# Two swiglu layers: four plain column pairs, then pairs of gate and up columns by seven half-size products

## The reference

```
h = rmsnorm(x, g_pre_ffn)                       # over the 1024 channels
g, u = split(h @ w_gu)                          # w_gu: 1024 x (2816 + 2816)
x = x + 0.5 * rmsnorm((silu(g) * u) @ w_down, g_post_ffn)   # w_down: 2816 x 1024
```

## Time and profile before

| what | value |
|---|---|
| median of three runs | 2426.96 us (2425.76 to 2429.64) |
| profiled execution, its own time | 2429.99 us |
| its span, first to last instruction | 2428.2 us |
| TensorE busy | 2366.4 us, 97% |
| VectorE busy | 1330.4 us, 55% |
| ScalarE busy | 1064.6 us, 44% |
| GpSimd busy | 233.4 us, 10% |
| DMA, mean over the span | 95 GB/s |

### The profile page before, as it was taken

One profiled execution on the slowest core, in us unless ns is written; L12 is line 12 of the kernel. 1 busy time (PEld: TensorE's weight loads), 2 busy tenths in 40 slices (PEclk: granted clock), 3 DMA queues, 4 the chain that ended last, 5 costly groups with the idle time before them and its releaser, 6 DMA issues.

```text
span 2428.2 us, 30842 instructions
## 1 busy us (share of the span) xinstructions
PE 2366.4 (97%) x12214; PEld 1941.6 (80%) x12214; DVE 1330.4 (55%) x2135; ACT 1064.6 (44%) x1759; POOL 233.4 (10%) x189
## 2 busy tenths in 40 slices
PE   8999999999999999999999999999999899999998
PEld 7888888777777788888887667989987677888987
DVE  5533436788654345432435866735645776753643
ACT  4323224455432334322323556614634785742642
POOL 0100100322102010100100300001001100000100
PEclk9999999999999999999999999999999999999999
DMA  4323223211122132323222214536532012744641
GB/s 145 100 87 109 95 87 100 85 53 53 61 70 72 55 117 70 104 86 114 88 86 88 86 44 130 148 104 160 136 96 74 29 47 72 172 115 125 150 122 64
DMA packets 72864, 230.68 MB, mean 95 GB/s; under 512 B 8080, under 2 KB 16528, under 8 KB 72464
## 3 DMA queue, kind: packets, MB, share of 16 engines
q1 hardware_dynamic: 66672, 206.68, 26.2%
q0 software_dynamic: 6048, 22.02, 5.5%
HBM read 226.57 MB, written 2.10 MB: 94 GB/s over the span
## 4 chain that ended last, share of the span: by engine, by line
PE 84%; DVE 6%; ACT 5%; issue 3%; DMA 2%; POOL 0%; POOLq 0%; SPq 0%; DVEq 0%; ACTq 0%
PE bank L2145 21%; PE bank L2149 21%; PE bank L2147 21%; PE bank L2163 3%; PE bank L2167 3%; PE bank L2165 2%; DMA wraw<-in_stream 2%; PE bank L2328 2%; ACT whi L2449 2%; DVE wlo L2791 1%; PE bank L2290 1%; PE bank L2335 1%; PE bank L2236 1%; PE bank L2232 1%; PE bank L2234 1%
## 5 line engine op out<-in xcount | busy, mean ns | idle before, releaser
L2791 DVE TENSOR_TENSOR wlo<-wraw,whi 128x1024 fp32r<-128x1024 f32 (+3 forms) x462 | 518.2, 1126 | 530.9 <-ACT whi L2449 529.6
L2449 ACT ACTIVATE whi<-wraw 128x1024 fp32r<-128x1024 f32 (+3 forms) x462 | 434.9, 948 | 472.6 <-PE bank L2149 374.6
L2145 PE MATMUL bank<-hhi,whi 128*128 128x512 f32 x1288 | 515.2, 400 | 6.6 <-ACT whi L2449 4.6
L2149 PE MATMUL bank<-hhi,wlo 128*128 128x512 f32 x1288 | 504.2, 391 | 1.6 <-DVE wlo L2791 1.5
L2147 PE MATMUL bank<-hlo,whi 128*128 128x512 f32 x1288 | 503.6, 391 | 0.4 <-DVE hlo L2839 0.4
L2145 PEld LDWEIGHTS bank<-hhi,whi 128*128 128x128 f32 x1288 | 242.4, 188 | 61.2 <-issue 6.4
L2149 PEld LDWEIGHTS bank<-hhi,wlo 128*128 128x128 f32 x1288 | 242.1, 188 | 55.7 <-DVE wlo L2791 4.0
L2147 PEld LDWEIGHTS bank<-hlo,whi 128*128 128x128 f32 x1288 | 242.6, 188 | 49.6 <-DVE hlo L2839 2.5
L2145 PE MATMUL bank<-mhi,whi 128*128 128x512 f32 x448 | 177.2, 396 | 0.0
L2147 PE MATMUL bank<-mlo,whi 128*128 128x512 f32 x448 | 177.0, 395 | 0.2 <-DVE mlo L3145 0.2
L2149 PE MATMUL bank<-mhi,wlo 128*128 128x512 f32 x448 | 177.0, 395 | 0.0
(11 more groups left out here) (459 smaller groups left out, 4221.1 us busy)
## 6 DMA issues: line engine op xcount, KB each, us to landing
wraw<-in_stream SPq DMA_DIRECT2D x335, 512.0 KB, 3.5
wraw<-in_stream POOLq DMA_DIRECT2D x34, 512.0 KB, 6.0
wraw<-in_stream SPq DMA_DIRECT2D x32, 192.0 KB, 2.4
wraw<-in_stream SPq DMA_DIRECT2D x22, 256.0 KB, 2.6
rot_tables<-in_stream SPq DMA_DIRECT2D x8, 512.0 KB, 5.6
rot_tables<-in_stream POOLq DMA_DIRECT2D x8, 512.0 KB, 5.5
wraw<-in_stream SPq DMA_DIRECT2D x26, 128.0 KB, 2.0
wraw<-in_stream SPq DMA_DIRECT2D x8, 320.0 KB, 3.0
```

Of the source, the lines that this page charges most:

```text
L2145: pe.matmul(out, sh, xh, start=first, stop=False)
L2149: p = pe.matmul(out, sl, xh, start=False, stop=end and last)
L2449: act.activation(whi[j][:, 0:L], src[:, 0:L], F.Copy).then_inc(*hi.up(c))
L2791: dve.tensor_tensor(wlo[j][:, 0:L], src[:, 0:L], whi[j][:, 0:L].bitcast(f32), SUB).then_inc(*lo.up(c))
```

## The change

- **Swiglu columns.** Features 0, 1, 2 and 11 stay plain (eight columns, all at the start of the layer). The other eighteen go two at a time through seven products each: `GATED`, four blocks in the first half (starting at features 3, 5, 7, 9), five in the second (12, 14, 16, 18, 20). The four columns of a block are the gate and the up columns of two features.
- `token_sums` and the product loop (`by_seven`) are taken out of `mlp` so that both layers use them; the order of mlp's own steps stays. In `ffn`, pieces 0 to 3 of the token sums stand between the gates of features 0, 1, 2 and 11.
- **The finish of a block** is new: per block two more multiplications by `rb` on VectorE, three multiplications on GpSimd (two of them by `rb`), two silus and two high copies on ScalarE.
- **Down columns** are begun as in mlp: the first two are interleaved with the last two products.
- **The rotary steps** move to the second half's down columns, two before each of the columns 0 to 4. Their position load on SyncE now waits for the last q7's split and for the two buffers they use. `rot_tables` serves as a third weight buffer in both swiglu layers.
- **SBUF**: 96 bytes of padding (`to_128_bytes`), and `qk`, `dl`, `xch` allocated ahead of the odd-sized tensors; each tensor named above then starts at a multiple of 128 bytes.
- **The start**: the first weights are SyncE's first load, the columns' table and x's first tile are loaded from ScalarE's queue, the identity comes last; TensorE runs 20 matmuls of 128x128 on `ones` first.

```diff
+PLAIN, GATED = (0, 1, 2, 11), ((3, 5, 7, 9), (12, 14, 16, 18, 20))
...
+    def ffn(s, tag, gu, down_of):
+        lows[s], least = [], len(plan) + 2
+        for f in PLAIN:
+            col(tag + "g", gu + "g", f)
+            col(tag + "u", gu + "u", f)
...
+            seven(tag + "s", s, GATED[half], lambda f: quadrants([gu + "g"] * 2 + [gu + "u"] * 2, (f, f + 1) * 2), down,
+                  least)
...
+                g0, u0, g1, u1 = side_by_side(("h", s), *[(tag + c, n, 0) for n in range(2) for c in "gu"], fresh=s > 0)
+                g2 = run(feat([(tag + "g", 2, 0)], ("h", s)))
                 R.step()
+                token_sums(s, 0, guard)
                 gate(s, 0, g0, u0, afree)
                 gate(s, 1, g1, u1, afree)
+                u2 = run(feat([(tag + "u", 2, 0)], ("h", s)))
+                token_sums(s, 1, guard)
+                gate(s, 2, g2, u2, afree)
+                token_sums(s, 2, guard)
+                g3 = run(feat([(tag + "g", 11, 0)], ("h", s)))
+                token_sums(s, 3, guard)
+                state["held"] = True
+                u3 = run(feat([(tag + "u", 11, 0)], ("h", s)))
+                put("token_last", s, u3.end)
+                gate(s, 11, g3, u3, (("p_lo", ("last token", s)),))
...
+            elif name == "q3":
+                low()
+                u = silu_of[f, "up"]
+                put("glu_gate", key, "c12", q.i)
+                put("glu_second", key, q.i, u.i)
...
+                if half and n < 5:
+                    next(extra, None)
+                    next(extra, None)
...
+        sb("to_128_bytes", [128, 24])
...
                 if k == "init":
-                    sp.dma_start(cols[:, 0:ncols], t["cols"]).then_inc(ld["cols"], 16)
+                    fetch(raws[0])
+                    sp.dma_start(xa[:, 1, :], t["x"][:, 1, :]).then_inc(ldx[1], 16)
+                    fetch(raws[1])
...
-                    w.wait_ge(ld["ident"], 16)
                     w.wait_ge(*ones_set[0])
-                    pe.matmul(banks[0][0:1, 0:1], ident[:, 0:1], ones[:, 0:1], start=True, stop=True)
+                    for _ in range(20):
+                        pe.matmul(banks[0][:, 0:128], ones[:, :], ones[:, :], start=True, stop=True)
...
+                    act.dma_start(cols[:, 0:ncols], t["cols"]).then_inc(ld["cols"], 16)
+                    act.dma_start(xa[:, 0, :], t["x"][:, 0, :]).then_inc(ldx[0], 16)
```

More of the change, by code:

```diff
@@ L567, in gate, with token_sums @@
         q.free = (("v_lo", (s, f)),)
[L569 to L572 removed]
+    first, both = FT.slots
+    def token_sums(s, k, guard):
+        qs = [T.take(), T.take()]
+        for q, j in zip(qs, (k, k + 4)):
+            put("plain", s, j, q.i, (*q.was, *x_at[j]))
+        put("token_sums", s, k, qs[0].i, qs[1].i, (*first.free, *both.free), guard)
+        for q in qs:
+            q.free = (("combined", ("token", s, k, 4)),)
+        put("token_parts", s, k, guard)
+        first.free = both.free = (("p_hi", ("token", s, k)), ("p_lo", ("token", s, k)))
@@ L592, in ffn, with tile @@
+            def tile(n):
+                return feat([(tag + f"d{half}", n, k0) for k0 in (0, 8)], ("v", s, half))
+            begun = [tile(0), tile(1)]
+            h_end = multiplied(GATED[half], begun, iter(()))
+            while wait_lo:
+                low()
             if half:
@@ L1256, in multiplied @@
-        def multiplied(fs, tiles, afree):
-            def nothing():
-                pass
-            later = nothing
-            for f, name in products(fs):
-                if name == "down":
-                    next(tiles[0])
-                    next(tiles[0])
-                    later()
-                    later = nothing
-                    continue
-                at_once, then = product(f, name, (*afree, *open_sums["h", s].tok) if f == 12 else afree)
-                later()
-                if (f, name) == (4, "p5"):
-                    put("token_last", s, ("used", CH[(f"m{l}u", 3, 0)]))
-                at_once()
-                state["held"] = False
-                later = then
-                if f > 4:
-                    next(owed, int)()
-            next(tiles[1])
-            next(tiles[1])
-            later()
-            return ("used", CH[(f"m{l}s", fs[-1], "q3")])
+            if part == "c21":
+                q = T.take()
+                put("corner", key, part, b.i, q.i, (done, *q.was), free)
+                b.free = (("relu_sq", (key, part, "relu")),)
+            else:
+                put("corner", key, part, None, q.i, (), free)
```

318 lines of the change are left out of this document (210 added, 108 removed).

## The result

| | median us | ratio to before | 95% interval |
|---|---|---|---|
| before, same comparison | 2426.36 (2423.76 to 2432.35) | | |
| changed | 2451.48 (2449.62 to 2456.38) | 1.0103 | 1.0093 to 1.0113 |

The changed kernel is slower by 25 us; 2419 with a range of 2388 to 2438 was predicted.

The account below looks back on a forecast made before the run. The prediction took TensorE, busy for 97% of the span, as the bound: number of matmuls times the distance of their starts. Its terms summed to -8.4 us, from the median 2426.96 to 2419 us, range 2388 to 2438.

Parts of the forecast that it names:

- products: Swiglu columns: eight plain columns and nine blocks of seven products replace 44 plain columns; -31.8 us for two layers.
- placement: About 3000 matmuls of 512 tokens read data now aligned to 128 bytes and start closer together; -19 us.
- sums of tokens: Matmuls of 256 tokens on `thi` in the blocks may go from 0.1179 to 0.1200 us apart; +2.4 us.
- start: Kernel start: earlier first weights load and matmuls on `ones` bring the full rate forward; -3 us.
- join: Where swiglu's plain columns meet products, p5 and p6 wait behind token pieces and gates; +36 us.
- inside halves: TensorE's waits inside the blocks of the four swiglu halves; +4 us, bounds 0 and 10.
- ends of halves: At each half's end the last corner passes up to 0.9 us late, four times; +3 us.
- the rival with a chance of 0.08: The larger distance between matmul starts belongs to the place in SBUF, not the 32 bytes; 2436 us, chance 0.08.
- The rival on adding transfers: Adding transfers come late in the five-block halves, 3 us per half more; 2431 us, chance 0.07.
- The first rival: The swiglu join costs what mlp's does, +8 in place of +36; 2391 us, chance 0.20.
- VectorE as the bound: Rival: VectorE becomes the bound in the swiglu blocks, at 21.5 us per block; 2446 us, chance 0.10.

Follow-up runs that it names:

- pad_only: Kernel before with only the change's SBUF part: 96 bytes of padding and qk, dl, xch allocated earlier; 2423.4 us, ratio 0.9986.
- start_only: Kernel before with only the change's start: new load order and 20 matmuls on ones first; 2424.9 us, ratio 0.9992.
- data_low: Kernel before with the two halves of SBUF exchanged, stage tensors low and still 32 bytes past a multiple of 128; 2427.7 us, ratio 1.0006.
- holds_before_splits: Changed kernel with the weight splits of q7 and the next q1 put behind the holds of p5 and p6 in swiglu blocks; 2445.8 us, ratio 1.0086.
- pad_224: Kernel before with pad_only's layout but 224 bytes of padding in place of 96; 2409.2 us, ratio 0.9923.
- all_160: Kernel before as weights_160, with data also moved by 32 bytes, all but v_end; 2414.7 us, a single execution.
- weights_160: Kernel before with 224 bytes of padding, weights' buffers behind hhi and hlo and moved by 32 bytes; 2448.2 us, ratio 1.0090.

## Why the prediction was wrong

Its terms against what the traces and runs gave:

| term | predicted | measured | from |
|---|---|---|---|
| products | -31.8 | -31.8 | 0.1188 apart, a block 20.0 |
| placement | -19 | -3.5 | pad_only |
| sums of tokens | +2.4 | +1.9 | 0.1187, 2304 matmuls |
| start | -3 | -1.8 | start_only |
| join | +36 | +34.9 | 17.4 and 17.5 per layer |
| inside halves | +4 | +18.1 | 8.7 and 9.4 per layer |
| ends of halves | +3 | +3.4 | four columns, 0.85 late each |
| sum | -8.4 | +21.2 | 19.6 between the profiles |

The last three are read from the profile of the changed kernel, as the time between starts of matmuls beyond 0.1187 us on sums of tokens, 0.1199 on `hhi` and 0.2267 or 0.2327 for 512 tokens. The 1.6 us between the two sums are less than the scatter of single executions.

**The step that failed first** is placement: "All the tensors listed as 32 bytes past show the second distance", and from it "-19". The contrast was exact and the property named was one of several that went with it. The listed tensors differ from hhi by 32 bytes, by place, and by their remainder against the weights' buffers, and only the last one counts in these runs. The bound named for this term, "0, if the distance comes from the place", was nearly met (-3.5), but not because the place counts, and the rival with a chance of 0.08 gave 2436. That this lies nearer to the measured 2451 than the forecast does is luck: the rival's mechanism, the place, is refuted by data_low, and the number leaves out the waits below. Place and 32 bytes were taken as the only two alternatives. With 224 bytes the term would have been right in size: -18.

**The second** is "For four halves +4 us", the waits inside the halves, sized by the two waits that mlp had the earlier trace rows; they cost 18.1. A swiglu block asks more of the order than an mlp block: a product by rb, a silu and a product on GpSimd between two corner steps, with the same four temporaries. I costed these steps as VectorE's load (15.3 of 20.0 us, measured 14.0) and not as a chain through ScalarE's queue, where the split that waits for the row sum stands ahead of two holds. The rival on adding transfers, at 3 us per five-block half, named a link of this chain; the whole chain costs 9 per layer, and how much of it the transfer causes is open. What holds_before_splits shows is the order: 5.7 of the 18.1 us go when the splits of q7 and q1 stand behind the holds.

**The join was right** in mechanism, and in its sum partly by luck. rb's end to p5's whi: 25.2 predicted, 24.2 measured; to p6's whi 36.9 and 35.4; to p6's end 40.8 and 41.6. Inside the sum two shares were off and cancelled: TensorE waits 10.8 us in the second layer and not 16.7, and matmuls in windows with a granted clock of 0.52 and 0.64 cost 6.7 (17.5 less the waits) and not 1.3. The first rival (a join as short as mlp's) did not occur. The start lost part of its gain to its own second load, x's first tile, which reached ScalarE 1.0 us later than before.

**VectorE as the bound** did not come: 14.0 us of 20.2. Beside GpSimd a split takes 2.48 us (1065.35 in the second layer) in place of 1.22. That is 1.26 us more, beside a GpSimd instruction of 1.60 that had 1.38 still to run; the split at 1061.61, beside one that had 0.39 still to run, took 1.48. By what means the one delays the other is not shown.

All in all the products save 32 us and the join, the blocks and the ends of halves give 56 back. Of the 33 us between 2419 and 2451 the placement is 15.5 and the waits inside the halves 14.1. Some 5 us are the difference between the profiles' 19.6 and the medians' 25, which lies in the scatter of single executions.

## What to carry to other kernels

A contrast between groups of tensors is a hint of many properties at once. List them all (address by 32, 128, 256 and 512 bytes, place against the other operand, order, producer) before pricing one, and give the term a low chance when no run separates them. A faster form with more feeding steps is worth its saving only where the feeders' queues have slack in the right order: price each wait of an engine that works through one list in order as a chain, from the step that waits to everything queued behind it, and count the buffers, because with none to spare a step can be neither earlier nor later. Count the slow clock on the matmuls that follow long waits: here, after waits of 5.3 and 2.75 us, it was 6.7 of the join's 17.5 us in the second layer.

## What the runs showed of the hardware

- Matmuls of 512 columns in reduced fp32: in the runs where weights and data have the same byte address by 512 in the partition, 24 on f1ahi and f1alo take 5.44 us, 0.2267 apart (pad_224, both at 128; all_160, both at 160). Where they have not, 24 take 5.58 to 5.60, 0.2326 to 0.2333 apart (weights at 128 and data at 0: 5.58 in pad_only and the changed kernel; data at 160: 5.60 in data_low; weights at 160 and data at 128: 5.60 in weights_160). By 256 bytes the same pairs agree and disagree. In weights_160 the weights alone move, and the matmuls on hhi slow from 5.44 to 5.60. What in the chip makes the difference no run here shows. On this kernel 128 bytes of padding are 14 us (pad_only to pad_224).
- Matmuls of 256 columns on the sums of tokens: 24 take 2.88 us, 0.1200 apart, in pad_224 and all_160, 2.83 (0.1179) in the kernel before and data_low, 2.85 (0.1187) in pad_only and the changed kernel.
- After waits of 5.29 and 2.75 us the granted clock was 0.64 over p5's 11.19 us and 0.52 over p6's 6.12 (the second layer of the changed kernel): 21 of p6's 24 matmuls of 256 columns, from 1025.90 on, start 0.21 us apart (20 distances in 4.27 us) in place of 0.1187.
- The SBUF address in this program is not the sum of the sizes: in the built programs the first tensor, xa, begins at byte 16512, and every start is a multiple of 32 (so `xch` is at 221632 in the kernel before, 64 past a multiple of 128 and not 48 as summed ahead). The 16512 bytes leave a remainder by 128 as it is, but a remainder by 512 has to be read from the built program.
